# Broadcast sums of the decay steps: fp32 products with ones, or fp32r products with ones of a high and a low part

## The reference

```python
g = -jnp.exp(a_log) * jax.nn.softplus(a + dt_bias)      # decay step per token and head
gcum = jnp.cumsum(_scalar_chunks(g), axis=-1)
diff = gcum[..., :, None] - gcum[..., None, :]
decay = jnp.exp(jnp.where(causal, diff, -jnp.inf))
m = jnp.where(strict, jnp.einsum('nbhik,nbhjk->nbhij', kb, kc) * decay, 0.0)
t_mat = lax.linalg.triangular_solve(eye + m, ..., lower=True, unit_diagonal=True)
qk = jnp.einsum('nbhik,nbhjk->nbhij', qc, kc) * decay
q_dec = qc * jnp.exp(gcum)[..., None]
```

## Time and profile before

| | us |
|---|---|
| median of 3 runs | 1071.06 (1070.56 to 1071.3) |
| the profiled execution, device time | 1071.28 |
| its span in the profile | 1069.5 |

### The profile page before, as it was taken

How to read it: one execution, slowest core, us unless ns; L and a number is a source line. 1 busy time by engine, 2 the same in 40 slices (tenths; PEclk the granted TensorE clock), 3 DMA queues, 4 the chain that set the end, 5 groups by cost and what they waited for, 6 DMA issues and landing times.

```text
span 1069.5 us, 16330 instructions
## 1 busy us (share of the span) xinstructions
PE 1061.2 (99%) x5966; PEld 871.7 (82%) x5966; DVE 718.7 (67%) x1030; ACT 465.9 (44%) x813; POOL 518.8 (49%) x387
## 2 busy tenths in 40 slices
PE   9999999999999999999999999999999999999997
PEld 7788888888888888888888888877788788888886
DVE  4887988248656666666685556458654678886863
ACT  6335411647443333333334445245554644344663
POOL 5445442233544444444456666533347677532551
PEclk9999999999999999999999999999999999999999
DMA  8963630520332323232323325322124322212222
GB/s 219 168 94 66 93 72 10 158 79 16 120 102 79 118 78 118 78 111 85 108 79 108 95 83 162 86 79 79 40 79 119 94 58 67 80 40 80 79 80 78
DMA packets 101773, 97.33 MB, mean 91 GB/s; under 512 B 4944, under 2 KB 95824, under 8 KB 101328
## 3 DMA queue, kind: packets, MB, share of 16 engines
q1 hardware_dynamic: 101424, 95.97, 32.3%
q10 hardware_dynamic: 288, 0.52, 0.1%
HBM read 94.38 MB, written 2.10 MB: 90 GB/s over the span
## 4 chain that ended last, share of the span: by engine, by line
PE 97%; DVE 1%; DMA 0%; ACT 0%; issue 0%; DVEq 0%; ACTq 0%
PE ps L2172 27%; PE ps L2174 27%; PE ps L2173 27%; PE ps L2789 4%; PE ps L2723 1%; PE ps L2734 1%; PE ps L2711 1%; PE ps L2474 1%; PE ps L2247 1%; PE ps L2486 1%; PE ps L2250 1%; PE ps L2253 1%; PE ps L2421 0%; DMA x_t<-in_x 0%; PE ps L2771 0%; PE ps L2517 0%
## 5 line engine op out<-in xcount | busy, mean ns | idle before, releaser
L624 POOL TENSOR_TENSOR w_lo<-raw,w_hi 128x512 fp32r<-128x512 f32 (+2 forms) x327 | 445.0, 1374 | 509.6 <-ACT w_hi L771 466.6
L771 ACT ACTIVATE w_hi<-raw 128x512 fp32r<-128x512 f32 x278 | 171.2, 627 | 180.6 <-PE ps L2174 165.3
L2172 PE MATMUL ps<-x_a,w_hi 128*128 128x512 f32 x592 | 238.2, 402 | 0.2 <-DVE x_a L1380 0.2
L2174 PE MATMUL ps<-x_a,w_lo 128*128 128x512 f32 x592 | 230.8, 390 | 0.0
L2173 PE MATMUL ps<-x_a,w_hi 128*128 128x512 f32 x592 | 230.7, 390 | 0.0
L2172 PE MATMUL ps<-x_b,w_hi 128*128 128x512 f32 x416 | 162.2, 390 | 0.0
L2174 PE MATMUL ps<-x_b,w_lo 128*128 128x512 f32 x416 | 161.8, 389 | 0.0
L2173 PE MATMUL ps<-x_b,w_hi 128*128 128x512 f32 x416 | 161.8, 389 | 0.0
L2172 PEld LDWEIGHTS ps<-x_a,w_hi 128*128 128x128 f32 x592 | 111.2, 188 | 30.6 <-issue 5.9
L2173 PEld LDWEIGHTS ps<-x_a,w_hi 128*128 128x128 f32 x592 | 111.3, 188 | 23.8 <-issue 2.2
L2174 PEld LDWEIGHTS ps<-x_a,w_lo 128*128 128x128 f32 x592 | 111.1, 188 | 23.6
(11 more groups left out here) (407 smaller groups left out, 1673.8 us busy)
## 6 DMA issues: line engine op xcount, KB each, us to landing
raw<-in_w_up SPq DMA_DIRECT2D x44, 512.0 KB, 4.0
raw<-in_w_in SPq DMA_DIRECT2D x28, 512.0 KB, 7.8
raw<-in_c_w_in SPq DMA_DIRECT2D x24, 512.0 KB, 4.6
raw<-in_a_w_in SPq DMA_DIRECT2D x18, 512.0 KB, 4.2
raw<-in_w_down SPq DMA_DIRECT2D x16, 512.0 KB, 4.4
raw<-in_w_out SPq DMA_DIRECT2D x8, 512.0 KB, 4.0
raw<-in_c_w_out SPq DMA_DIRECT2D x8, 512.0 KB, 4.2
raw<-in_w_down SPq DMA_DIRECT2D x8, 384.0 KB, 3.4
```

What stands on the lines that cost most here:

```text
L624: nc.gpsimd.tensor_tensor(ring_half(WL, n), raw_half(n), f32(ring_half(WH, n)), SUB) \
L771: nc.scalar.activation(ring_half(WH, n), raw_half(n), ACT.Copy).then_inc(w_hi, 1)
L2172: mm(out, w_hi_, x_hi_, start=first, stop=False)
L2174: return mm(out, w_lo_, x_hi_, start=False, stop=last)
```

## The change

The broadcast sum is made of two fp32r products for each bank instead of one fp32 product. VectorE rounds the decay steps to fp32r (`GGH`), takes the rest (`GGL`), and multiplies the mask with each: 16 blocks of the high part into the place of `T`, 16 of the low part into the place of `M`. TensorE waits for both. The matrix of ones is declared fp32r and read as fp32 by all its other users.

```diff
@@ -178,7 +178,8 @@
         AR = 65536
         G = 204800
         IDENT = at("ident", [P, P], F32, G)
-        ONES = at("ones", [P, P], F32, G + 512)
+        ONESR = at("ones", [P, P], F32R, G + 512)
+        ONES = ONESR[:, :].bitcast(F32)
         RSTD = at("rstd", [P, S], F32, G + 1024)
         ACC = at("acc", [P, S], F32, G + 3072)
         PAR = at("params", [P, NPAR], F32, G + 5120)
@@ -197,6 +198,8 @@
         GT = at("gates", [P, 8, S], F32, AR + 32768)
         M = at("m", [P, NB * H, P], F32, AR + 32768)
         T = at("t", [P, NB * H, P], F32, AR + 40960)
+        GUH = at("decay_steps_hi", [P, NB * H, P], F32R, AR + 40960)
+        GUL = at("decay_steps_lo", [P, NB * H, P], F32R, AR + 32768)
         TT = at("tt", [P, NB * H, P], F32, AR + 49152)
         QKT = at("qkt", [P, NB * H, P], F32, AR + 57344)
         GRAM = at("k_gram", [P, NB * H, P], F32, AR + 57344)
@@ -238,6 +241,9 @@
         XS = at("row_spread", [P, NB * H, BK], F32, AR + 73728 + 5120)
         XP = at("row_product", [P, NB * H, BK], F32, AR + 73728 + 6144)
         GG = SM[:, 2, :]
+        SMR = at("small_r", [P, 12, 16], F32R, G + 7264)
+        GGH = SMR[:, 5, :]
+        GGL = SMR[:, 4, :]
         BETA = SM[:, 3, :]
         RKN = SM[:, 0, :]
         VBETA = SM[:, 1, :]
@@ -1608,8 +1614,12 @@
                                                 op0=MUL, op1=MUL))
                     step(v.tensor_scalar(SPB, SPB, 1.0, None, ADD))
                     step(v.reciprocal(BETA, SPB))
-                    v.tensor_tensor(T[:, :, :], UPPER.unsqueeze(1).broadcast_to([P, 16, P]), lastdim(GG), MUL) \
-                        .then_inc(gu_ready, 1)
+                    step(v.tensor_copy(GGH, GG))
+                    step(v.tensor_tensor(GGL, GG, f32(GGH), SUB))
+                    v.tensor_tensor(GUH[:, :, :], UPPER.unsqueeze(1).broadcast_to([P, 16, P]), lastdim(f32(GGH)),
+                                    MUL).then_inc(gu_ready, 1)
+                    v.tensor_tensor(GUL[:, :, :], UPPER.unsqueeze(1).broadcast_to([P, 16, P]), lastdim(f32(GGL)),
+                                    MUL).then_inc(gu_ready, 1)
                     dve.wait_ge(g_copied, 1)
                     step(v.tensor_tensor(DIAG[:, :, :], GRAM[:, :, :],
                                          IDENT[:, :].unsqueeze(1).broadcast_to([P, 16, P]), MUL))
@@ -2586,13 +2596,15 @@
                     ins.then_inc(g_filled, 1)
                 if u == 13:
                     pe.wait_ge(g_copied, 1)
-                    pe.wait_ge(gu_ready, 1)
+                    pe.wait_ge(gu_ready, 2)
                     mm(PS[:, 4, 0:16], UPPER, GG, start=True, stop=True).then_inc(gc_filled, 1)
                     for c in (1, 2, 3, 0):
                         if c == 0:
                             pe.wait_ge(gc_ready, 1)
-                        ins = mm(PS[:, 4 + c, :], ONES[:, :],
-                                 T[:, 4 * c:4 * c + 4, :].rearrange("p h i -> p (h i)"), start=True, stop=True)
+                        mm(PS[:, 4 + c, :], ONESR[:, :],
+                           GUH[:, 4 * c:4 * c + 4, :].rearrange("p h i -> p (h i)"), start=True, stop=False)
+                        ins = mm(PS[:, 4 + c, :], ONESR[:, :],
+                                 GUL[:, 4 * c:4 * c + 4, :].rearrange("p h i -> p (h i)"), start=False, stop=True)
                     ins.then_inc(gcb_filled, 1)
                 if u == 14:
```

## The result

| | before | after |
|---|---|---|
| median, us (20 runs each) | 1070.88 (1069.97 to 1071.37) | 1072.56 (1071.84 to 1073.94) |
| ratio after / before | | 1.0017, 95% interval 1.0012 to 1.0023 |
| profiled execution, us | 1071.28 | 1072.61 |
| its span | 1069.5 | 1070.8 |

The changed kernel is 1.7 to 1.8 us slower, near 0.17% and so just inside the 0.2% that I called no change. TensorE's busy time fell only from 1061.2 to 1061.0, and VectorE's rose from 718.7 to 724.6.

A forecast was written before the change was run, and what follows sets the result against it. TensorE, busy 99% of the span, was taken to bound the kernel. TensorE's end moves 2.55 - 0.48 = +2.07 us, containing the +1.19 at the copy: 1071.28 + 2.07 - 0.22 = 1073.1 us, range 1070.9 to 1074.9.

The forecast's parts named there:

- TensorE's work: Products of ones: eight fp32r products at 0.23 take 1.84 us instead of 3.52, a gain of 1.68.
- VectorE's list: Added VectorE steps and low part (2.29 us) ahead of the Gram diagonal: diagonal taken up at 90.99, 1.73 later.
- VectorE and GpSimd in turn: At the Gram diagonal: GpSimd's waiting split of half 29 goes first, adding 1.17 us; the copy ends at 96.81.
- The first stop: TensorE before its product c = 0: idle 2.87 us waiting for the copy, next unit starts 1.19 later.
- The alternation behind it: L1631 to L1640: four GpSimd splits alternate with VectorE's products; L1640 ends at 115.45 instead of 112.90, 2.55 us late.
- The transfer: Transfer started by split 35 moves by 2.55 us; TensorE's wanted half is 0.3 to 0.8 late beyond the 1.19.
- The step that failed: L1640 to first inversion level: VectorE stays 2.55 us late; less 0.48 slack, TensorE ends 2.07 later.
- The clock rival: TensorE's clock drops to its lower level after the 2.9 us idle: 1.9 more, 1075.0 us; chance 0.10.
- The other side: Copy not late, as if VectorE made the two products at 1.08 instead of 2.29 us: 1069.4; chance 0.04.

The follow-up runs named there:

- the two reordered kernels: Changed kernel and kernel before, each with four steps put elsewhere (small copy, rotation tables, splits of halves 29 to 31): 1069.81 and 1071.37 us.
- the reordered fp32 kernel: Kernel before, fp32 products, with four steps put elsewhere (small copy, rotation tables, splits of halves 29 to 31): 1071.37 against 1070.76 us, ratio 1.0008.

## Why the prediction was right

The direction, the size within half a microsecond and the mechanism held; one of its last steps did not. Point by point:

- **TensorE's work.** 0.23 a product; gain 1.68 forecast, 1.64 in the run without the low part's VectorE work, which is the clean measurement; the 1.56 to 1.72 between the two reordered kernels holds waits of its own.
- **VectorE's list.** The diagonal was taken up at 90.84. The forecast was 90.99, which is 90.85 in this execution, whose first Gram product starts 0.14 earlier. The low part costs what L1611 cost.
- **VectorE and GpSimd in turn.** The waiting split went ahead, and the diagonal took 3.38. Forecast end of the copy 96.81 - 0.14 = 96.67, measured 96.61. Removing the waiting split removed the 1.09. The Trainium skill (SBUF — State Buffer, section "Who interferes with whom") gives the exclusive hold; the order among those that wait, longest first, is what the rows here add.
- **The first stop.** Forecast +1.19, measured +1.11: the copy ended 0.06 sooner than forecast, and the restart behind it was 0.02 quicker.
- **The alternation behind it.** Ten instructions ahead, L1650 was put at 115.45 - 0.14 = 115.31; it ended at 115.12.
- **The transfer.** Put at "0.3 to 0.8 late beyond the 1.19", measured 0.37.
- **The step that failed** is "From L1640 to the first level VectorE has next to no idle time, so its 2.55 stays". The first masked block of the first level started at 146.40 against 144.58, with the 0.14 a lateness of 1.96. VectorE has no idle time there, but it has time lost to GpSimd, which depends on how the two meet: a small product that met a split took 1.32 before (at 122.68) and only 0.92 after (at 124.03), which gives back 0.4, and L1650 was already 0.2 earlier than forecast: 2.55 - 0.6 = 1.95. At 1.96 less the slack of 0.48, VectorE could have asked for +1.48, and TensorE was at +1.53 for the transfer. So the transfer set the end, not the level, and the total was +1.46 to +1.53 in the profiled execution where I had put 2.07. The forecast's own transfer term, 1.19 + 0.3 to 0.8, holds this value; the sum went by the level. That the two limits ended 0.05 apart is luck, and it is why the wrong one cost the forecast so little. Against the median, the forecast of 1073.1 was 0.5 too high: 0.4 is this step (2.07 against +1.68), and 0.2 the median of before, which came out at 1070.88 where I had 1071.06.
- **The clock rival.** It was given 0.10 for the idle at the copy. In the profiled execution the granted clock behind that idle was full. Two of the twenty executions took 1073.8 and 1073.9 at a mean clock of 0.997 against 0.999 for most; that they lost it at this place was not seen, and one execution of the reordered fp32 kernel, whose profile has no idle at the copy, took 1073.98 at 0.996. The rival's mechanism is real: behind an idle of 4.76 the half clock cost 2.3, where 1.9 was put. Its reading of the start was an inference from the pace alone, for the record of the granted clock is 1.00 from 0 to 8 us; and the record is not full throughout, it is at 0.50 in the last 3 us.
- **The other side.** Its mechanism (a VectorE product at the fast pace) was not there. But its time is reached when the VectorE work is hidden by other means.

VectorE's small product that met a split, before, then after, and its first masked block of the first level after (the earlier trace rows has it at 144.58):

```profile
122.68 1.32 DVE L1525 TENSOR_TENSOR row_product<-row_spread,blocks 128x64 f32<-128x64 f32 x1
```

```profile
124.03 0.92 DVE L1531 TENSOR_TENSOR row_product<-row_spread,blocks 128x48 f32<-128x48 f32 x1
...
146.40 0.90 DVE L1482 TENSOR_TENSOR xz<-ps,masks 128x128 f32<-128x128 f32 x4
```

ScalarE's high part of half 39, before and after:

```profile
121.92 0.63 ACT L771 ACTIVATE w_hi<-raw 128x512 fp32r<-128x512 f32 x1 [2.09 <-PE ps L2174]
```

```profile
122.89 0.63 ACT L777 ACTIVATE w_hi<-raw 128x512 fp32r<-128x512 f32 x1 [2.09 <-PE ps L2184]
```

These two rows show why the meeting changed: ScalarE's row, and GpSimd's split behind it, move with TensorE (0.97, with the 0.14 the +1.11), while VectorE's small products beside it had moved by twice as much.

## What to carry to other kernels

A cheaper product on the engine that bounds the kernel paid here only where what it needs was made out of its way: 3.5 us of products were cut to 1.8 and 2.7 us of work went in front of a copy for which the same products wait. Before moving work onto VectorE, look for GpSimd instructions that would become ready while it runs; in these runs each that waited went ahead of VectorE's next instruction with two SBUF operands and added its own length, 1.1 for a split. Freeing one wait showed nothing until the chain behind it (VectorE and GpSimd in turn, a split, a transfer) was shortened too.

## What the runs showed of the hardware

- VectorE's products with two SBUF operands and GpSimd's splits ran one after the other, and in turn when both waited: a split of 128x512 added 1.1 to the next such VectorE product. A VectorE instruction with a PSUM operand kept its 2.28 beside two splits (after the change L1656 at 115.24, splits from 115.20), and so did the sum before the change (L1616 at 91.59, 2.29, beside the split that ends at 92.72).
- An earlier transfer made a kernel slower: there 3.1 us sooner counted from the first Gram product (128.05 - 82.91 against 131.66 - 83.44), it let two splits meet VectorE's products and cost an idle of 2.3 and the half clock behind it.
- TensorE's granted clock fell to 0.50, its lower level of 1.2 GHz, during an idle of 4.76 between products of 128x512; it was full again by 104, with work since 98.34. It also fell after an idle of only 2.34 that stood between two groups of 64x32 products, some 0.4 into the second; after the idle of 2.44 between groups of 128x512 products it did not, in the profiled executions. At that level the products of 128x512 start every 0.43 instead of 0.23.
- In the run with half 30 split early, four of eleven executions had a lower mean clock and took 1.2 to 3.1 us more than the median of the others. The idle at the copy is the same as in the changed kernel, where it was two of twenty. The reordered fp32 kernel had one of eleven without that idle. Why the shares differ stays open.
